# A hybrid encoder step on one core: the rotation's half exchange by transfers, and six moves in a hand-woven order

## The reference

```python
h = rms_norm(x, norm1_g) * (1 + scale1) + shift1
u = h @ w_in                    # all heads' inputs, one projection
gdn_out, ... = gdn_mixer(g_qkv, g_a, g_b, g_gate, conv_w, ...)   # width-4 causal conv, silu, gated delta rule, chunk 64
q, k = rotary(a_q, pos), rotary(a_k, pos)                        # halves of 32: x1*cos - x2*sin, x2*cos + x1*sin
qi, ki = rotary(a_qi, pos), rotary(a_ki, pos)                    # indexer
score = sum_h wi * relu(qi . ki);  sel = top_k(score, 256)       # per query
att = softmax over the selected keys of (q . k) @ v
ssm_out, ... = ssd_mixer(s_z, s_xbc, s_dt, conv_w, conv_b, ...)  # width-4 causal conv, silu, SSD, chunk 64
x = x + gate1 * (concat(gdn_out, att, ssm_out) @ w_out)
x = x + gate2 * ((silu(conv(h2 @ w_gate) + b) * (h2 @ w_up)) @ w_down)
```

## Time and profile before

| | us |
|---|---|
| median of 3 runs | 4491.47 |
| lowest, highest | 4491.46, 4493.82 |
| the profiled execution's own time | 4497.23 |
| its span, first to last instruction | 4495.4 |
| PE busy | 4086.0 (91%) |
| DVE busy | 2255.5 (50%) |
| ACT busy | 1029.1 (23%) |
| POOL busy | 68.8 (2%) |

### The profile page before, as it was taken

One profiled execution on the slowest core, in us unless ns is written; L12 is line 12 of the kernel. 1 busy time (PEld: TensorE's weight loads), 2 busy tenths in 40 slices (PEclk: granted clock), 3 DMA queues, 4 the chain that ended last, 5 costly groups with the idle time before them and its releaser, 6 DMA issues.

```text
span 4495.4 us, 54493 instructions
## 1 busy us (share of the span) xinstructions
PE 4086.0 (91%) x21348; PEld 2293.8 (51%) x21348; DVE 2255.5 (50%) x4568; ACT 1029.1 (23%) x2145; POOL 68.8 (2%) x128
## 2 busy tenths in 40 slices
PE   5999888688989999999989998977889799999996
PEld 2545554457545555545545455544575455554553
DVE  3246566655344445454542565565562444444445
ACT  2134444234210000000021344442350100000001
POOL 0000000000000000000000000000000000000000
PEclk8999999789989999999999999987999899999998
DMA  4124111123121322121121121111231111111211
GB/s 196 47 101 149 45 50 38 62 100 123 34 86 66 113 97 92 38 80 38 39 92 58 44 69 50 56 65 57 83 120 40 70 41 45 38 38 38 80 33 56
DMA packets 112880, 311.28 MB, mean 69 GB/s; under 512 B 9456, under 2 KB 57264, under 8 KB 104816
## 3 DMA queue, kind: packets, MB, share of 16 engines
q1 hardware_dynamic: 101392, 253.06, 16.2%
q0 software_dynamic: 10368, 40.58, 2.3%
q10 hardware_dynamic: 864, 14.16, 0.7%
HBM read 253.03 MB, written 54.47 MB: 68 GB/s over the span
## 4 chain that ended last, share of the span: by engine, by line
PE 83%; DVE 8%; DVEq 3%; ACT 2%; issue 2%; ACTq 1%; DMA 1%; SPq 0%; POOL 0%; POOLq 0%
PE PS L1287 34%; PE PS L803 15%; PE PS L1280 6%; PE PS L1328 3%; PE PS L783 2%; DVE big L1793 2%; DVE hT L1793 2%; PE PS L1364 2%; PE PS L1216 2%; PE PS L905 1%; PE PS L731 1%; PE PS L1236 1%; PE PS L970 1%; DVE big L1790 1%; PE PS L981 1%
## 5 line engine op out<-in xcount | busy, mean ns | idle before, releaser
L803 PE MATMUL PS<-hT,ring 128*128 128x512 f32 (+1 forms) x2304 | 844.6, 512 | 0.0
L803 PEld LDWEIGHTS PS<-hT,ring 128*128 128x128 f32 x2304 | 372.5, 196 | 318.3 <-issue 306.8
L1287 PE MATMUL PS<-hT,ring 128*128 128x512 f32 x832 | 372.4, 600 | 16.8 <-ACTq L1430 10.4
L1287 PE MATMUL PS<-xT 128*128 128x512 f32 x704 | 314.7, 601 | 24.2 <-DVEq L2500 24.2
L1287 PE MATMUL PS<-hT,xT 128*128 128x512 f32 x704 | 310.5, 594 | 0.0
L1287 PEld LDWEIGHTS PS<-hT,ring 128*128 128x128 f32 x832 | 159.1, 193 | 221.4 <-issue 220.9
L1280 PE MATMUL PS<-big,ring 128*128 128x512 f32 (+1 forms) x768 | 252.6, 489 | 0.0
L1545 ACT ACTIVATE big<-xT,tk 128x896 bf16<-128x896 f32 (+2 forms) x192 | 231.7, 1207 | 51.5 <-DVEq L1966 44.0
L1287 PEld LDWEIGHTS PS<-xT 128*128 128x128 f32 x704 | 135.8, 193 | 196.3 <-issue 196.3
L1949 DVE TENSOR_SCALAR_CACHE_REDUCE big<-xT,tk 128x384 bf16<-128x384 f32 (+5 forms) x262 | 215.1, 821 | 26.5 <-issue 1.3
L1397 ACT ACTIVATE big<-big 128x1152 f32<-128x1152 f32 x72 | 83.8, 1164 | 559.5 <-DVEq L2633 544.9
(11 more groups left out here) (374 smaller groups left out, 5351.5 us busy)
## 6 DMA issues: line engine op xcount, KB each, us to landing
big<-in_w_ada SPq DMA_DIRECT2D x80, 512.0 KB, 6.2
ring<-in_w_in SPq DMA_DIRECT2D x54, 512.0 KB, 3.5
scr<-big POOLq DMA_DIRECT2D x40, 576.0 KB, 3.1
ring<-in_w_gate SPq DMA_DIRECT2D x44, 512.0 KB, 3.6
ring<-in_w_up SPq DMA_DIRECT2D x44, 512.0 KB, 4.5
hT<-in_kcache SPq DMA_DIRECT2D x16, 1024.0 KB, 6.2
hT<-in_vcache SPq DMA_DIRECT2D x16, 1024.0 KB, 6.9
ring<-in_w_down SPq DMA_DIRECT2D x32, 512.0 KB, 4.2
```

What stands on the lines that cost most here:

```text
L803: x = mm(PS[:, o:o + m], w[:, k, :], hT[:, k, c0:c0 + m], start=(k == 0), stop=(k == KT - 1))
L1287: i = mm(bank(b), w[:, k, :], x[:, k, :], start=(k == 0), stop=(k == n - 1))
```

## The change

Seven things are done in one edit.

- The rotation's exchange: behind its copy to `ext`, ScalarE issues four transfers of 32 partitions each (`swap_halves`) from `ext` to the tile's place in `rot`; VectorE multiplies by the sine and by a column of signs, in SBUF. `rotate`, its waits and its matmuls go. Two semaphores `rot_in` count the transfers. TensorE's waits for `rotated` become waits for the evacuation.
- One tap of the convolution, the last with the bias, is made by ScalarE from PSUM at the evacuation (three chunks); VectorE makes three, at h = 1 to 3. ScalarE now waits there for the earlier store of the same buffer.
- The masks become the last 14 places of lane B, in the projections; lane M, its table and the waits of single blocks go, and attention waits once for all. They work in the search's own buffers.
- Early search: 40 places of B, not 27, stand in the stretch before G begins.
- The output transposes: the first tile's behind the product `z` of the next state step, the second's behind the row sums of the next pair; G has 27 places per pair, not 28, and 92 of them, not 96, are in D's stretch.
- D's tail has two places, not seven.
- The ring loads of two more weight tiles are issued in D's places; SP no longer waits for the masks.

```diff
-MASK_HOPS = (0, 0, 1, 1, 3, 3, 4, 4, 5, 5, 6, 6, 7, 7, 8, 8) + tuple(range(10, 14)) + tuple(range(16, 20)) + tuple(range(22, 26))
...
-        G_HOPS = 4 * (5 + 10 + 12 + 1) + (5 + 6 + 5)
+        G_HOPS = 4 * (5 + 10 + 12) + (5 + 6 + 5)
...
-        B_HOPS = 3 * 32 + 2
-        D_HOPS = ND * DH + 7
+        B_HOPS = 3 * 32 + 1 + 14
+        D_HOPS = ND * DH + D_TAIL
...
-        B_A = 27
-        G_D = 96
+        B_A = 40
+        G_D = 92
         order = weave(D=DH) + weave(D=I_HOPS, I=I_HOPS) + weave(D=D_I, A=A_HOPS, B=B_A) + \
-            weave(D=D_HOPS - D_A, G=G_D, B=B_HOPS - B_A) + masked(weave(G=G_HOPS - G_D, T=T_HOPS)) + weave(S=S_HOPS)
+            weave(D=D_HOPS - D_A, G=G_D, B=B_HOPS - B_A) + weave(G=G_HOPS - G_D, T=T_HOPS) + weave(S=S_HOPS)
...
-                            if h == 1 and i + 6 < NPROJ + 2:
+                            if h == 1:
                                 load_pos(i + 6)
                             yield
-                    for h in range(7):
+                    load_pos(ND + 6)
+                    for h in range(D_TAIL):
                         yield
...
-                sp.wait_ge(*mask_ready.at(l, 7))
-                for n in range(NPROJ + 2, NPROJ + KT):
+                for n in range(NPROJ + 4, NPROJ + KT):
                     load_pos(n)
...
-                            if h == 3 and i and tile_kind(D_TILES[i - 1]) == "rot":
-                                pe.wait_ge(*proj_evac.at(l, 3 * i + 3))
-                                pe.wait_ge(*rotated.at(l, i + 2))
-                                rotate(i + 2, ext_user(i - 1) % 2, 0)
...
                     if n == 2:
-                        pe.wait_ge(*rotated.at(l, 1))
+                        pe.wait_ge(*proj_evac.at(l, 1))
                     project(n, w).then_inc(*proj_done.up())
-                    if n:
-                        pe.wait_ge(*proj_evac.at(l, n))
-                        rotate(n - 1, (n - 1) % 2, (n - 1) % 2)
...
                         if q:
-                            pe.wait_ge(*g["out"].at(l, 2 * q))
+                            pe.wait_ge(*g["oe"].at(l, 2 * q))
...
                         i.then_inc(*g["row"].up())
+                        if q:
+                            turn_out(PAIRS[q - 1][1])
                         yield
                         pe.wait_ge(*g["sq"].at(l, q + 1))
+                        if q:
+                            pe.wait_ge(*g["out"].at(l, 2 * q))
...
                                 if p == 1 and c == 0:
-                                    turn_out(pair[0])
+                                    pe.wait_ge(*g["oe"].at(l, t))
...
                                 i.then_inc(*g["z"].up())
+                                if p == 1 and c == 0:
+                                    turn_out(pair[0])
                                 yield
...
-                        turn_out(pair[1])
-                        yield
...
-                        if t in MASK_TILES and hp == 0 and c == 0:
-                            pe.wait_ge(*mask_ready.at(l, 1 + MASK_TILES.index(t)))
+                        if t == PT0 and hp == 0:
+                            pe.wait_ge(*mask_ready.at(l, 1))
...
+                def swap_halves(n):
+                    for o in (0, 64):
+                        for x, y in ((o, o + 32), (o + 32, o)):
+                            sc.dma_start(rot[x:x + 32, ROT_SLOT[n], :], ext[n % 2][y:y + 32, 0:TOK]).then_inc(*rot_in[n % 2].up())
...
-                    act_(dst, src, ACT.Copy).then_inc(*proj_evac.up())
+                    if kind == "conv":
+                        if c == 0:
+                            if tile_kind(D_TILES[i - 2]) == "rot":
+                                sc.wait_ge(*rotated.at(l, i + 2))
+                            sc.wait_ge(*act_stored[i % 2].at(l, stores_before(i)))
+                        q = D_TILES[i] - LEAD
+                        act_(dst, src, ACT.Copy)
+                        act_(cout[i % 2][:, c0:c0 + m], PS[:, o:o + m], ACT.Identity, scale=par[:, P_CW + q * 4 + 3:P_CW + q * 4 + 4],
+                             bias=par[:, P_CB + q:P_CB + q + 1])
+                        dr().then_inc(*proj_evac.up())
+                        return
+                    act_(dst, src, ACT.Copy)
+                    dr().then_inc(*proj_evac.up())
+                    if c == 2:
+                        swap_halves(i + 3)
...
-                def turn_sin(n, s_, c):
-                    dv.wait_ge(*rot_done.at(l, n + 1))
+                def turn_sin(n, c):
+                    dv.wait_ge(*rot_in[n % 2].at(l, 4 * (n // 2 + 1)))
                     r_ = rot[:, ROT_SLOT[n], :]
-                    tt_(r_, pset(s_), csn[:, 1, :], ALU.mult)
+                    stt(r_, r_, sign[:, 0:1], csn[:, 1, :], ALU.mult, ALU.mult)
...
-                            if kind == "conv" and 1 <= h <= 4:
+                            if kind == "conv" and 1 <= h <= 3:
                                 conv_tap(D_TILES[j], e, c, h - 1)
```

More of the change, by code:

```diff
@@ L44 @@
 ND, DH = len(D_TILES), 9
+D_TAIL = 2
 ROT_SLOT = (4, 5, 6, 0, 1, 2, 3)
@@ L262, in build @@
         proj_evac = signal("proj_evac", 3 + 3 * ND)
-        rot_done = signal("rot_done", NROT)
+        rot_in = [signal(f"rot_in{p}", 4 * (4 - p), 16) for p in range(2)]
         rotated = signal("rotated", NROT)
@@ L631, in gdn_sp @@
                                 load_q(t, p)
-                        for i in range(24 if q < 4 else 12):
+                        for i in range(23 if q < 4 else 12):
                             yield
@@ L907, in _, with turn_out @@
                     i.then_inc(*vn_done.up())
-                    if t == 2:
-                        pe.wait_ge(*proj_evac.at(l, 3))
-                        rotate(2, 0, 0)
+                def turn_out(t):
+                    pe.wait_ge(*g["on"].at(l, t + 1))
+                    ot = gbuf[0]["ot"].rearrange("p h v -> p (h v)")
+                    for hp in range(2):
+                        i = nc.tensor.transpose(PS[:, 768 + hp * 128:896 + hp * 128], ot[:, hp * 128:(hp + 1) * 128], ident)
+                    i.then_inc(*g["ot"].up())
                 def gdn_pe():
@@ L987, in gdn_pe @@
                             break
-                        def turn_out(t):
-                            pe.wait_ge(*g["on"].at(l, t + 1))
-                            ot = d["ot"].rearrange("p h v -> p (h v)")
-                            for hp in range(2):
-                                i = nc.tensor.transpose(PS[:, 768 + hp * 128:896 + hp * 128], ot[:, hp * 128:(hp + 1) * 128],
-                                                        ident)
-                            i.then_inc(*g["ot"].up())
                         for p, t in enumerate(pair):
@@ L1520, in proj_act @@
                     for i in range(ND + 1):
-                        for h in range(DH if i < ND else 7):
+                        for h in range(DH if i < ND else D_TAIL):
                             if i == 0 and h == 0:
@@ L1554, in bisect_act @@
                         yield
-                    yield
+                    for i in range(14):
+                        yield
                 def gdn_act():
@@ L1774, in _ @@
             V.memset(one_t[:, :], 1.0)
+            V.memset(sign[:, :], 1.0)
+            dr()
+            for r in (0, 64):
+                V.memset(sign[r:r + 32, :], -1.0)
             for i in range(2):
@@ L2028, in bisect_dve @@
                     as_float(FB, T)
-                    yield
-                spare = ring[:, (l * R_ALL + NPROJ + 2) % 4:(l * R_ALL + NPROJ + 2) % 4 + 2, :].rearrange("p a b -> p (a b)")
-                sel, scan = spare[:, 0:520].bitcast(bf16), spare[:, 520:1560]
-                def masks_dve():
-                    dv.wait_ge(*proj_done.at(l, 3 + 3 * ND))
-                    for j in MASK_ORDER:
+                    for j in range(7):
                         n = SC_N[j]
@@ L2085, in proj_dve @@
                                 conv_begin(D_TILES[j], e)
-                            if kind == "conv" and 1 <= h <= 4:
+                            if kind == "conv" and 1 <= h <= 3:
                                 conv_tap(D_TILES[j], e, c, h - 1)
-                            if kind == "conv" and h == 5:
+                            if kind == "conv" and h == 4:
                                 conv_tail(D_TILES[j], e)
@@ L2132, in ada_dve, with gate_out @@
                     yield
+                def gate_out(t, gate, b0):
+                    stt(mixT[:, 0:2, t * 128:(t + 1) * 128], PS[:, b0:b0 + 256].rearrange("p (h t) -> p h t", h=2),
+                        par[:, P_GNG:P_GNG + 1], gate, ALU.mult, ALU.mult).then_inc(*g["out"].up())
                 def gdn_dve():
@@ L2218, in gdn_dve @@
                                 i.then_inc(*g["r"].up())
-                                if p == 1 and c == 0:
-                                    dv.wait_ge(*g["ot"].at(l, t))
```

(6 more changed lines are left out.)

72 lines of the change are left out of this document (27 added, 45 removed).

## The result

The changed kernel takes 4320.44 us (median of 4 runs, 4319.62 to 4323.34) against 4492.65 for the kernel before (4 runs beside them): a ratio of 0.9616, 95% interval 0.9599 to 0.9632. The profiled execution took 4319.62 us with a span of 4317.8.

What follows compares the result with a forecast made beforehand. TensorE, 83% of the span's chain, was taken as the bound, with its waits read by stage. Terms 16.8 + 12 + 18 + 4 = 50.8 us per layer, 102 for two, gave 4390 us; range 4325 to 4450.

Steps and rivals of the forecast that it cites:

- Masks and the end of the search: Moved from attention to among projections: 39.9 us leave, 22 are paid there, net 18 us per layer.
- The clock: Attention's first 66 us at granted clock 0.64: 10 us less at 0.86, left out of the sum.
- Rotation: Projections: seven rotations leave TensorE, where it is the bound; 16.8 us per layer gained.
- Output turns: Transposes of outputs in the woven stretch: 9 of 21.3 us of waits stay, gain 12 per layer.
- Tail places: Empty projection places at the end, 7 to 2: more cover for lane G, 4 us per layer.
- Early search and the tap: Search places ahead of lane G and a convolution tap on ScalarE: hidden, costing and bringing nothing.
- The woven stretch at 387 us, a few either way: Sign of being right: the stage weaving projection, search and gated DeltaNet keeps its length.
- Attention ... about 195: Sign of being right: attention falls from 236 to about 195 us, with diagonal waits under 10.
- Rival 2: All mask work is covered and attention's clock recovers: 78.8 us per layer, 4334 us; chance 0.18.
- Rival 1: Masks only change place, exposed by in-order waits: 23.8 us gained per layer, 4444 us; chance 0.18.
- Rival 3: The rotation's swaps land late and hold VectorE: 34 us gained per layer, 4423 us; chance 0.05.
- Rival 4: Slower: mask places among projections run at the lower clock, 6 us per layer lost, 4504 us; chance 0.09.

Runs made afterwards that it cites:

- rotation and masks alone: Kernel before with rotation by transfers and the masks' move, without early search, later turns, shorter tail and ScalarE's tap: 4349.95 us, ratio 0.9682.
- Masks twice: Changed kernel with VectorE making all mask pieces a second time at their old places in attention, results unused: 4442.84 us, ratio 0.9883.
- the filler: Kernel before with 24 idle matmuls in attention ahead of each wait for the diagonal but the first: 4492.43 us, ratio 0.9993.

## Why the prediction fell short

**The step that failed** is the term "Masks and the end of the search ... Net: 39.9 - 22 = 18 us". Alone, the move was worth 49 us in layer 0 (98 to 104 us in all), 31 more than that. Two of its inputs failed: the clock, put at nothing, and the price of the new places, put too high. Its three parts:

- *What leaves attention.* 39.9 us of waits were forecast; 33.6 us of idle time left with the masks' move. That part was 6 us too large.
- *The clock, "left out of the sum".* This is the main miss: 24.4 us of TensorE's busy time in layer 0, with the same matmuls. An estimate of 10 us was made for the 66 us at 0.64 alone, taken up to the neighbour's 0.86; but that neighbour was itself slowed by the same waits, and all of attention now has 0.95 (0.97 with rotation and masks alone). (Some matmul records are missing, 1561 against 1536 in these two windows. Between before and after, with 1572 and 1598 recorded, the fall is 24.7.) Masks twice (+23.1) and the filler (-19.8) put much the same price on it from two other sides.
- *What the masks cost at their new places.* 22 us were taken; alone it was 8 (5 in layer 1). In that run TensorE still stands 20.0 us at the output transposes, as in the earlier trace rows, and VectorE may do the masks meanwhile; this was argued from the overlap of the other parts, not run by itself.

Together 33.6 + 24.4 - 8.1 = 50 by the windows, 49 by the stages' own marks.

**Point by point, the rest.**

- *Rotation*, 16.8 us per layer: 20.0 measured to lane G's start, and 18.8 in layer 1 from its first projection on. The end of V's projection came 11.0 us earlier instead of 9. The transfers land in 2.6 us at the median, where 3.1 was taken; an issue takes 0.61 us of ScalarE, where 0.33 was. VectorE waits for transfers ahead of four of the seven sine products (three of them in the first projections), 20.5 us together and 10.5 at the very first, whose transfers took 7.6 to 9.8 us; TensorE waits behind none: its only waits from 60 to 150 us are 3.7 us for the first activations and 2.0 us for the modulation.
- *Output turns*, 12: the wait fell by 15.2 us, and undone alone they cost 15 us per layer.
- *Tail places*, 4: 5 by the medians, uncertain (6.3 us of the woven stretch in layer 0, nothing in layer 1).
- *Early search and the tap, "nothing"*: wrong in the changed kernel (10 and 8.5 us per layer when undone there, 13 together). Beside turns that are not moved they do bring nothing: with the turns alone undone, and with all four undone, the time is the same. Nor are the two layers alike here, as the prediction took them to be: in layer 1 early search delays lane G by some 10 us and gains 15.6 behind it. That the sum of the four terms came out (15 per layer against 16) is luck: their prices overlap, and the turns bring 15 only if search and tap are out of the way too (3 with the tail where these are undone).
- *Masks in the full change*: the mask places cost 15.8 us of the woven stretch (13 taken), and with the end of the search 14.7 (22 taken): the two don't add.
- *"The woven stretch at 387 us, a few either way"*: 374.8. *"Attention ... about 195"*: 178.2, the clock's 24.7 us less the 7.6 of waits that stayed (32.3 us of idle time gone, 39.9 forecast).

**The rivals.** Rival 2 (all covered, the clock recovers, 4334) was nearest, by the right mechanism and with too small a price for the clock. Rival 1 did not come: of the masks' 40.1 us at most 15.8 show. Rival 3 did not, with 2.6 us to landing. Rival 4 did not, but its mechanism shows: the last 86 us of the woven stretch, with the mask places, have a clock of 0.82 (0.88 in the last 89 us before the change), above the 0.69 at which it would have decided. The rival of the study, that the small parts made the gain, fell with rotation and masks alone: 147 us of the 172, each by the medians of its own comparison (4496.85 - 4349.95, 4492.65 - 4320.44).

## What to carry to other kernels

Where an engine waits in many places of a stage and its clock there is below that of its neighbours, price the stage twice: the waits, and the busy time at the clock of a neighbour with fewer of them (with the 0.93 of the woven stretch, 184.2 us x 0.81/0.93 = 160 here, 159.5 measured). A part that costs nothing beside a stall costs its price once the stall is removed, so terms of one stage are to be summed in the order in which the stalls go. Work that moves beside another engine's matmuls may be worth cutting into short places: the same masks in 21 places instead of 14, with the search's end in four, gave 31 us more.

## What was not expected of the hardware

TensorE's other matmuls in attention ran 19.8 us faster in sum when 27.2 us of useless ones were put in front of its waits, at a granted clock of 0.91 instead of 0.81. With TensorE's idle time down by 13.4 us the stage is 5 us shorter in layer 0 and 3 longer in layer 1, and the whole shows no difference. Twenty-eight transfers per layer between partitions of SBUF, 144 KB each, landed in 2.6 us at the median (2.3 to 9.8), below the 3.3 us of a store of 576 KB to HBM in the same execution.
